# Early products for eight expert pairs, and a step-size projection with its weights held

## The chip, the cores and the metric

The kernel runs on one core of a Trainium2 chip. The metric is the time of one execution on the device in microseconds (us); lower is better. Engines are named as in the profile: PE is TensorE (PEld its weight loads), DVE is VectorE, ACT is ScalarE, POOL is GpSimd, SP is SyncE, which issues most of the transfers.

## The reference

One layer of a diffusion backbone for 640 tokens (128 context tokens, 512 latent ones), model width 1024:

```
h = modulate(rmsnorm(x, norm1), shift1, scale1)
z, xbc, dt_f, dt_b, q, k, v, g_a, g_b = split(h @ w_in)      # dt_f, dt_b: 32 step sizes each
dt = softplus(dt + bias); y_a = ssd_scan(xbc, dt, ...) ; y_b = attention(q, k, v)
x = x + gate1 * (sigmoid(g_a) * y_a + sigmoid(g_b) * y_b) @ w_o
h = modulate(rmsnorm(x, norm2), shift2, scale2)
s = (h @ w_pq) . sub_keys                                    # 8 heads x 2 x 128 scores
gate, idx = softmax of the best 16 sums of a first and a second key, for each head
x = x + gate2 * sum_k gate_k * gelu(h . u_tab[idx_k]) * v_tab[idx_k]   # 16384 experts
y = rmsnorm(x, final_norm)
```

An expert is named by two keys of 128, so 16384 experts are 64 "pairs" of 256 (two first keys, all second keys).

## The kernel before

The program is a row of phases with a barrier between them: modulate, tokens (q, k, v and step sizes), attention, SSD, the merge and output projections, mix_out, route, gates, experts. Weights come from HBM in units of 1 MB (`w_stream`). Each unit is split into a rounded high part (ACT, `w_hi`) and a remainder (DVE, `w_lo`), and a product is three matmuls: high x high, high x low, low x high, all in the chip's rounded 32-bit type (fp32r). Two raw buffers, two high and two low ones take turns.

**modulate and tokens.** In modulate PE transposes the normed tokens, projects the conditioning vector in two halves (L280, `ps_row`), and ACT scales and shifts the transposed tokens tile by tile into `hf` (L207); DVE splits each tile (L221, L223). tokens then begins on PE with the step sizes `t_row`: for each of 5 token tiles and 8 slices of the width three matmuls in which the token tile is the held operand and the 64 columns of weights stream through (L115 to L117, 120 matmuls), and then unit 0 of q, k, v (`t_ps`). DVE's softplus chain (from L535) and ACT's exponentials need all of `t_row`.

**route.** For each of 8 heads h PE makes the queries (`r_ps`, L1848, 96 matmuls) and the scores (`r_pk`, L1858). ACT does, in this order, `copies(h+1)` of the queries (L1889) with the next unit's high part (L100), `score_copies(h)` (`r_sc`, L1898) and `gate_exp(h-1)`: two replicas of the found keys (`r_fr`, L1906) and an exponential (`r_be`, L1911). DVE searches one head after another: two rounds of eight best from the scores (from L1943), the found keys as `r_f` (L1960), the sum candidates, then `r_eq` times `r_fr` (L1985), then `r_be` (L1990), and at the end the low part of the unit of head h+4 (L105).

**gates.** 48 groups of 8 latent tokens become one-hot matrices (DVE, POOL), PE multiplies them into a dense 128 x 128 gate matrix for each token (`e_ps`, L2071), ACT evicts into one of two stages `e_st` of 64 tokens, and SP writes a full stage, 4 MB, to `g_dram` (6 writes, L2039). A stage may be filled again when its write is done.

**experts.** The 384 latent tokens behind the first 256 go through all 64 pairs densely, while the first 256 tokens take their 128 chosen experts each by indirect gathers from HBM, one slot after another: POOL issues `p_uv` (L2188, 256 gathers of 1 MB into a ring of 8), DVE makes the dot product (L2337), and later adds the weighted row to `ysum` (L2351, shown as `merged`, `v_done`). PE alternates `hidden(n+1)` (48 matmuls of 384 columns into `p_pa`) and `output(n)` (36 of 512 columns into six accumulators `p_py`). DVE's step is fixed in the code:

```
dot(n, s, 0, t); weight(n, s); dot(n, s, 1, t)
split_lo(unit_u, 1); w_lo(n, s)          # u of pair n+1; low part of the gated activations
dot(n, s, 2, t); dot(n, s, 3, t)
split_lo(unit_v, 0)                      # v of pair n
slot_weight(n, s, t)
for j in range(GS): take(n, s, j, t)     # GS = 4 slots a pair
```

ACT's split of the v unit waits for `output(n-1)`, since it overwrites that buffer. The gates of a pair are read from `g_dram` as 768 pieces of 512 bytes (L2143). The loops over pairs are hardware loops of two pairs each.

Of the kernel before, what the change touches and what calls it, by code (L numbers as in the profile page):

```python
# [23 lines left out]
P = 128  # L24
# [33 lines left out]
N_EXP = 128  # L58
# [63 lines left out]
def phase_modulate(nc, K, ctx):  # L122
# [9 lines left out]
    hf = sb("hf", [P, 2, KD, P])  # L132
    sq = sb("sq", [P, D])
# [5 lines left out]
    modc = sb("modc", [P, 16, 2])  # L139
    ps_row = ctx.enter_context(nc.psum_tensor("ps_row", [P, 2 * UC], F32))  # L140
# [7 lines left out]
    xn_done = sem("m_xn"); xT_done = sem("m_xT"); hf_done = sem("m_hf"); hhi_done = sem("m_hhi"); hlo_done = sem("m_hlo")  # L148
# [3 lines left out]
    with nc.Block() as block:  # L152
# [32 lines left out]
        def _(act):  # L185
# [5 lines left out]
            for t in range(NT):  # L191
                if t:
                    act.wait_ge(sq_done, t)
                nc.scalar.activation(sq[:, :], xt[:, t, :], ACT.Square, accum_out=ssq[:, t:t + 1]).then_inc(sq_done, 1)
            act.wait_ge(ms_done, 1)
            nc.scalar.activation(rstd[:, :], ssq[:, :], ACT.Sqrt).then_inc(rt_done, 1)
            act.wait_ge(ada_used, 2)
            nc.scalar.activation(row[:, :], ps_row[:, :], ACT.Copy).then_inc(row_done, 1)
            act.wait_ge(scale_done, 4)
            for t in range(NT):  # L200
                for h in range(2):
                    act.wait_ge(xT_done, 2 * t + h + 1)
                    if t >= 2 and h == 0:
                        act.wait_ge(hlo_done, t - 1)
                    for k in range(4):
                        kd = 4 * h + k
                        nc.scalar.activation(hf[:, t % 2, kd, :], ps_x[t % 3][h][:, k, :], ACT.Identity,  # L207
                                             scale=K.mul1[:, kd, group(t):group(t) + 1],
                                             bias=K.add1[:, kd, group(t):group(t) + 1]).then_inc(hf_done, 1)
                if t == 0:  # L210
                    S.hi(act, 0, 0)
                if t == 2:
                    act.wait_ge(dtw_in, 16)
                    nc.scalar.activation(K.whi[1][:, 0:KD * 64], dtw[:, :], ACT.Copy).then_inc(dtw_hi, 1)

        @block.vector
        def _(dve):
            def split(t):

                dve.wait_ge(hf_done, KD * (t + 1))  # L220
                nc.vector.tensor_copy(K.hT[0][:, :, t * P:(t + 1) * P], hf[:, t % 2, :, :]).then_inc(hhi_done, 1)  # L221
                dve.wait_ge(hhi_done, t + 1)
                nc.vector.tensor_tensor(K.hT[1][:, :, t * P:(t + 1) * P], hf[:, t % 2, :, :],  # L223
# [2335 lines left out]
```

## Time and profile before

| | |
|---|---|
| median of 3 runs | 2925.51 us (2924.32 to 2927.39) |
| the profiled execution | 2930.75 us, its span 2929.0 us |
| PE / DVE / ACT / POOL busy, share of the span | 88% / 76% / 39% / 25% |
| experts, by its first and last matmul | 1814.94 to 2907.2 us |
| mean granted clock of PE | 0.93 of full speed |

The span counts from the first to the last instruction; 1.75 us of the execution lie around it. Times below are microseconds from the start of the span. The clock is a share of 2.4 GHz: 1.00 or 0.50.

### The profile page before, as it was taken

Reading aid. Unit: us, or ns where it says so; the run is one execution under the profiler, and the core shown is the slowest. Engines: PE = TensorE matmul, PEld = TensorE weight load, DVE = VectorE, ACT = ScalarE, POOL = GpSimd, SP = SyncE. Lnnn points to the kernel's source line nnn. Section 1 sums busy time; section 2 is a strip of 40 time slices with the busy share of each in tenths; the row PEclk is TensorE's granted clock in tenths of the full one; section 3 lists DMA queues with packets and bytes.
Section 4 is the critical chain, followed back from the end, with each engine's and each line's share of the span. In section 5 each row is a group of like instructions: output and inputs, shape, how many; then the busy total and the mean of one; then the engine's idle time right before and its main releaser. Section 6 shows DMA issues by size and latency. Waiting matters only on the chain. (4 is left out here: it accounts for less than half of the span.)

```text
span 2929.0 us, 41321 instructions
## 1 busy us (share of the span) xinstructions
PE 2562.9 (88%) x15289; PEld 2287.0 (78%) x15289; DVE 2211.7 (76%) x3790; ACT 1144.4 (39%) x1857; POOL 729.5 (25%) x588
## 2 busy tenths in 40 slices
PE   4979999978999998798786078899999999999997
PEld 3967878768887786797686078799899898899896
DVE  2565666661488787433399996899999999999998
ACT  3223445452466565321432176333333333333333
POOL 0000000000456676010000066223323333323221
PEclk7889999999999999899898589999999999999998
DMA  5430211123223231432211036999999999999996
GB/s 231 171 139 17 80 62 66 61 94 112 90 97 118 76 100 61 158 128 106 94 44 37 7 133 260 413 410 403 403 402 396 400 400 398 380 402 397 403 399 242
DMA packets 152003, 614.43 MB, mean 210 GB/s; under 512 B 13344, under 2 KB 77632, under 8 KB 89792
## 3 DMA queue, kind: packets, MB, share of 16 engines
q1 hardware_dynamic: 114720, 344.22, 31.7%
q0 software_dynamic: 36864, 268.45, 22.3%
q8 instruction: 80, 1.31, 0.2%
q14 instruction: 51, 0.42, 0.0%
q10 hardware_dynamic: 288, 0.03, 0.0%
HBM read 556.24 MB, written 56.41 MB: 209 GB/s over the span
## 5 line engine op out<-in xcount | busy, mean ns | idle before, releaser
L2188 POOL DMA_INDIRECT p_uv<-in_uv_rows,merged x256 | 332.7, 1300 | 733.6 <-DVE merged L2351 658.9
L2208 PE MATMUL p_pa<-h2D,w_hi 128*128 128x384 f32 x1024 | 346.7, 339 | 5.9 <-DVE w_lo L2315 3.6
L2210 PE MATMUL p_pa<-h2D,w_lo 128*128 128x384 f32 x1024 | 345.9, 338 | 0.0
L2209 PE MATMUL p_pa<-h2D,w_hi 128*128 128x384 f32 x1024 | 345.7, 338 | 0.0
L2245 ACT ACTIVATE w_hi<-w_raw 128x2048 fp32r<-128x2048 f32 x126 | 241.4, 1916 | 266.1 <-PE p_py L2224 241.0
L2351 DVE SCALAR_TENSOR_TENSOR merged<-p_uv,p_sw,merged 128x1024 f32<-128x1024 f32 x256 | 331.0, 1293 | 9.2
L2337 DVE CUSTOM_DVE_ANT_0 p_uv<-p_uv,merged 128x1024 f32<-128x1024 f32 x256 | 309.8, 1229 | 19.6 <-DMA p_uv<-in_uv_rows,merged 19.6
L2222 PE MATMUL p_py<-w_hi,p_wh 128*128 128x512 f32 x768 | 303.8, 396 | 12.8 <-DVE w_lo L2315 12.8
L2315 DVE TENSOR_TENSOR w_lo<-w_raw,w_hi 128x2048 fp32r<-128x2048 f32 x126 | 288.6, 2290 | 29.1 <-ACT w_hi L2245 29.0
L2223 PE MATMUL p_py<-w_lo,p_wh 128*128 128x512 f32 x768 | 303.4, 395 | 0.0
L2224 PE MATMUL p_py<-w_hi,p_wl 128*128 128x512 f32 x768 | 303.3, 395 | 0.0
L105 DVE TENSOR_TENSOR w_lo<-w_raw,w_hi 128x2048 fp32r<-128x2048 f32 x64 | 153.8, 2404 | 135.0 <-ACT w_hi L100 134.8
L2252 ACT ACTIVATE p_a<-p_pa 128x384 f32<-128x384 f32 x128 | 62.9, 492 | 358.6 <-PE p_pa L2210 358.6
L2208 PEld LDWEIGHTS p_pa<-h2D,w_hi 128*128 128x128 f32 x1024 | 194.0, 189 | 9.5 <-issue 5.6
L790 PE MATMUL c_pp<-hT,w_hi 128*128 128x320 f32 x1024 | 198.6, 316 | 0.0
L2209 PEld LDWEIGHTS p_pa<-h2D,w_hi 128*128 128x128 f32 x1024 | 194.0, 189 | 2.3
L2210 PEld LDWEIGHTS p_pa<-h2D,w_lo 128*128 128x128 f32 x1024 | 193.8, 189 | 0.0
L2222 PEld LDWEIGHTS p_py<-w_hi,p_wh 128*128 128x128 f32 x768 | 144.3, 188 | 45.3 <-DVE w_lo L2315 13.1
L1134 POOL TENSOR_TENSOR s_pv<-s_pv,decay 128x256 f32<-128x256 f32 x48 | 41.5, 865 | 536.2 <-ACT s_st L1295 535.1
L2224 PEld LDWEIGHTS p_py<-w_hi,p_wl 128*128 128x128 f32 x768 | 144.3, 188 | 34.9
L2223 PEld LDWEIGHTS p_py<-w_lo,p_wh 128*128 128x128 f32 x768 | 144.3, 188 | 32.3
L100 ACT ACTIVATE w_hi<-w_raw 128x2048 fp32r<-128x2048 f32 x64 | 122.6, 1915 | 112.4 <-PEq L1563 68.5
(368 smaller groups left out, 6049.6 us busy)
## 6 DMA issues: line engine op xcount, KB each, us to landing
w_raw<-in_w_stream SPq DMA_DIRECT2D x190, 1024.0 KB, 6.8
g_dram<-e_st SPq DMA_DIRECT2D x6, 4096.0 KB, 13.0
p_g<-g_dram SPq DMA_DIRECT2D x64, 384.0 KB, 6.5
t_ada<-in_w_ada SPq DMA_DIRECT2D x16, 1024.0 KB, 10.3
xc_dram<-c_xc SPq DMA_DIRECT2D x8, 1284.0 KB, 4.5
s_xx<-xc_dram SPq DMA_DIRECT2D x8, 642.0 KB, 6.0
s_bc<-xc_dram SPq DMA_DIRECT2D x8, 642.0 KB, 7.7
gate_dram<-s_gst SPq DMA_DIRECT2D x16, 320.0 KB, 6.1
```

What stands on the lines that cost most here:

```text
L790: mm = nc.tensor.matmul(ps_p[:, h, 0:TH], lhs[:, k, cols], rhs[:, k, h * TH:(h + 1) * TH], start=f, stop=l)
L2188: nc.gpsimd.indirect_dma_start(uv[:, k % RING, :], None, K.uv_rows, bass.IndirectOffsetOnAxis(K.sidx[:, t, c:c + 1], 0)).then_inc(K.gather ...
L2208: nc.tensor.matmul(ps_a[m][:, :], wh[:, k, cols], K.h2D[0][:, k, :], start=k == 0, stop=False)
L2209: nc.tensor.matmul(ps_a[m][:, :], wh[:, k, cols], K.h2D[1][:, k, :], start=False, stop=False)
L2210: mm = nc.tensor.matmul(ps_a[m][:, :], wl[:, k, cols], K.h2D[0][:, k, :], start=False, stop=k == KD - 1)
L2222: nc.tensor.matmul(ps_y[o][:, :], Wh[s][:, c, tc], vh[:, c, dc], start=first and c == 0, stop=False)
L2223: nc.tensor.matmul(ps_y[o][:, :], Wh[s][:, c, tc], vl[:, c, dc], start=False, stop=False)
L2224: mm = nc.tensor.matmul(ps_y[o][:, :], Wl[s][:, c, tc], vh[:, c, dc], start=False, stop=last and c == 1)
L2245: nc.scalar.activation(K.whi[slot][:, :], K.raw[slot][:, :], ACT.Copy).then_inc(K.w_hi_done, 1)
L2315: nc.vector.tensor_tensor(K.wlo[slot][:, :], K.raw[slot][:, :], K.whi[slot][:, :].bitcast(F32), ALU.subtract).then_inc(K.w_lo_done, 1)
L2337: nc.vector.tensor_tensor_reduce(uv[:, b, 0:D], uv[:, b, 0:D], K.hrow[:, t, :], 1.0, 0.0, ALU.mult, ALU.add, sa[:, b:b + 1]).then_inc(dot_ ...
L2351: nc.vector.scalar_tensor_tensor(ys[:, t, :], uv[:, b, D:2 * D], sw[:, b:b + 1], ys[:, t, :], ALU.mult, ALU.add).then_inc(v_done, 1)
```

## The change

Four parts.

1. **Step sizes.** The transposed tokens are kept in one tile `xT` (evicted unscaled while the conditioning weights still arrive, then scaled in place slice by slice), DVE splits by slices of the width, and PE projects the step sizes still in modulate, slice by slice, with the 64 weight columns held and 320 tokens streamed: 48 matmuls. tokens begins with 5 transposes of the result.
2. **Early pairs.** Eight pairs (4, 11, ..., 53) leave the stream. Their first products are made in route, two halves of 8 matmuls behind each head's scores, in plain fp32 (`r_pu`, from `ur` and the unsplit tokens `h32`, which mix_out now leaves), with a gelu each on ACT and a trip through `a_dram`. In experts 56 plain pairs remain; after pairs `r` = 4 to 51, in cycles of 6, PE adds 3, 3, 2, 2, 2 and 0 of an early pair's 12 output matmuls (fp32, 512 columns, `p_ve` by `p_ae`).
3. **Slots.** The 256 gather slots are spread over 56 steps: 4 each at the ends, 5, 5, 5, 4, 5, 4 in a cycle. The step's order changes, activations are gated in place, and the hardware loops are unrolled.
4. **Gates by row pairs.** The first 4 of 6 stages are written as 512-byte pieces so that a pair reads them as 2 KB a partition; the last 2 as before. The final gates and norm weights are loaded at the end of experts, not at its start.

```diff
+EARLY = {n: i for i, n in enumerate(range(4, 60, 7))}
+PAIR_OF = [n for n in range(NPAIR) if n not in EARLY]
 # modulate
+            for kd in range(KD):
+                pe.wait_ge(hlo_done, kd + 1)
+                for lhs, rhs, first, last in ((dtwh, K.hT[0], kd == 0, False), (dtwh, K.hT[1], False, False), (dtwl, K.hT[0], False, kd == KD - 1)):
+                    for h in range(2):
+                        mm = nc.tensor.matmul(ps_x[0][h][:, :, :].rearrange("p a c -> p (a c)")[0:64, 0:TH], lhs[:, kd, :],
+                                              rhs[:, kd, h * TH:(h + 1) * TH], start=first, stop=last)
 # tokens
             for t in range(NT):
-                tc = slice(t * P, (t + 1) * P)
-                for kd in range(KD):
-                    mm = mm3(nc, ps_dt[:, t, :], (K.hT[0][:, kd, tc], K.hT[1][:, kd, tc]),
-                             (dtwh[:, kd, :], dtwl[:, kd, :]), kd == 0, kd == KD - 1)
+                mm = nc.tensor.transpose(ps_dt[:, t, :], dtT[0:64, t * P:(t + 1) * P], K.ident[0:64, 0:64])
 # route, PE and ACT
+            for h in range(PH):
+                if h + 1 < PH:
+                    queries(h + 1, (h + 1) % 2)
+                scores(h, h % 2)
+                for i in behind(h):
+                    early_hidden(i)
...
+                    copies(h + 1, (h + 1) % 2)
+                score_copies(h, h % 2)
+                for i in behind(h)[:2]:
+                    early_gelu(i)
+                if h:
+                    gate_exp(h - 1)
 # gates
+                if b < G_PAIRED:
+                    rows = K.g_pairs[:, :, b].rearrange("n j i t -> j n (i t)")
+                    sp.dma_start(rows, stage[b % 2][:, :, :].rearrange("p (n i) t -> p n (i t)", i=2)).then_inc(out[b % 2], 16)
 # experts, PE and DVE
+            for r in range(R):
+                if r + 1 < R:
+                    hidden(r + 1)
+                output(r)
+                if early_of(r) and early_of(r)[1] < CYCLE - 1:
+                    early_output(*early_of(r))
...
+                first = COUNT[r] - 2
+                dot(r, 0)
+                weight(r)
+                dot(r, 1)
+                if r and r < R - 1:
+                    split_lo(u_unit(r + 1))
...
+                for j in range(2, first):
+                    dot(r, j)
+                w_lo(r)
+                slot_weight(r, 0)
+                for j in range(first - 1):
+                    take(r, j)
+                dot(r, first)
+                dot(r, first + 1)
+                if r < R - 1:
+                    split_lo(v_unit(r))
+                take(r, first - 1)
+                slot_weight(r, 1)
+                take(r, first)
+                take(r, first + 1)
```

In route, ACT's order in one head (`r_q` are the queries, `r_sc` the scores, `r_fr` the replicas for the head before, `r_be` its exponential). Before, in the loop:

```order
L1889 ACTIVATE r_q<-r_ps 128x256
L1889 ACTIVATE r_q<-r_ps 128x384
L1889 ACTIVATE r_q<-r_ps 128x256
L1889 ACTIVATE r_q<-r_ps 128x384
L100 ACTIVATE w_hi<-w_raw 128x2048
L1898 ACTIVATE r_sc<-r_pk 128x512 x2
L1898 ACTIVATE r_sc<-r_pk 128x256
L1906 ACTIVATE r_fr<-r_f 128x1280 x2
L1911 ACTIVATE r_be<-r_bs 128x80
```

and of the change, with the replicas of head 0:

```order
L1935 ACTIVATE r_q<-r_psS 128x256
L1935 ACTIVATE r_q<-r_psD 128x384
L1935 ACTIVATE r_q<-r_psS 128x256
L1935 ACTIVATE r_q<-r_psD 128x384
L106 ACTIVATE w_hi<-w_raw 128x2048
L1944 ACTIVATE r_sc<-r_pk 128x512 x2
L1944 ACTIVATE r_sc<-r_pk 128x256
L1964 ACTIVATE r_ua<-r_pu 128x384 x2
L1952 ACTIVATE r_fr<-r_f 128x1280 x2
L1957 ACT_TABLE_LOAD
L1957 ACTIVATE r_be<-r_bs 128x80
```

Two gelus (`r_ua`), whose input `r_pu` PE makes behind the scores, stand ahead of the replicas, and a table load ahead of the exponential; another comes before the next head's gelus.

In experts, DVE's step from the gating to the weighted sums (the rows with ISA are the dot products, `merged` is `ysum`). Before, with its four slots:

```order
L2325 TENSOR_TENSOR p_w<-p_a,p_g 128x384 x2
L2337 ISA p_uv,p_sa<-p_uv,merged 128x1024
L2337 ISA p_sa 128x1
L2315 TENSOR_TENSOR w_lo<-w_raw,w_hi 128x2048
L2331 TENSOR_TENSOR p_wl<-p_w,p_wh 128x768
L2337 ISA p_uv,p_sa<-p_uv,merged 128x1024
L2337 ISA p_sa 128x1
L2337 ISA p_uv,p_sa<-p_uv,merged 128x1024
L2337 ISA p_sa 128x1
L2315 TENSOR_TENSOR w_lo<-w_raw,w_hi 128x2048
L2342 TENSOR_TENSOR p_sw<-p_sg,merged 128x4
L2351 SCALAR_TENSOR_TENSOR merged<-p_uv,p_sw,merged 128x1024 x4
```

and of the change, in the first step of a cycle (five slots), from the split of the u unit on:

```order
L2399 TENSOR_TENSOR w_lo<-w_raw,w_hi 128x2048
L2428 ISA p_uv,p_sa<-p_uv,merged 128x1024
L2428 ISA p_sa 128x1
L2421 TENSOR_TENSOR p_wl<-p_a,p_wh 128x768
L2435 TENSOR_TENSOR p_sw<-p_sg,merged 128x3
L2445 SCALAR_TENSOR_TENSOR merged<-p_uv,p_sw,merged 128x1024 x2
L2428 ISA p_uv,p_sa<-p_uv,merged 128x1024
L2428 ISA p_sa 128x1
L2428 ISA p_uv,p_sa<-p_uv,merged 128x1024
L2428 ISA p_sa 128x1
L2399 TENSOR_TENSOR w_lo<-w_raw,w_hi 128x2048
L2445 SCALAR_TENSOR_TENSOR merged<-p_uv,p_sw,merged 128x1024
```

Two of the weighted sums now stand between the two splits, and the slots are weighted in two parts (`p_sw` of 3, and of 2 behind this piece). Ahead of this step the early pair was gated.

## Rows read from the trace of the kernel before

**Rows 1.** The page: the span.
```profile
span 2929.0 us, 41321 instructions
```

**Rows 2.** Windows: busy time, clock, DMA share and GB/s of two stretches.
```profile
core 0: us, PE busy (x) PEld busy (x) DVE busy (x) ACT busy (x) POOL busy (x), PEclk, DMA share, GB/s
61.00:87.00 26.00, 25.87 (x121) 25.90 (x122) 0.77 (x2) 1.54 (x2) 3.96 (x9) 0.50 0.47 184
1846.00:2895.00 1049.00, 1045.26 (x5229) 942.29 (x5230) 1010.70 (x1129) 353.06 (x374) 331.06 (x250) 1.00 1.00 398
```

**Rows 3.** Waits from 1846 to 2895 us: total, times, longest.
```profile
DVE w_lo L2315 <- ACT w_hi L2245: 29.0, 60, 2.3
ACT w_hi L2245 <- DMA w_raw<-in_w_stream: 25.1, 19, 3.0
```

**Rows 4.** Timeline of PE: begin of a hidden and of the output behind it.
```profile
2207.83 0.34 PE L2208 MATMUL p_pa<-h2D,w_hi 128*128 128x384 f32 x1
...
2216.16 0.39 PE L2222 MATMUL p_py<-w_hi,p_wh 128*128 128x512 f32 x1
```

**Rows 5.** Timeline of DVE, one step of experts and the next step's begin.
```profile
2200.91 1.22 DVE L2337 CUSTOM_DVE_ANT_0 p_uv<-p_uv,merged 128x1024 f32<-128x1024 f32 x1
2202.06 1.02 DVE L2325 TENSOR_TENSOR p_w<-p_a,p_g 128x384 f32<-128x384 f32 x2
...
2204.14 2.29 DVE L2315 TENSOR_TENSOR w_lo<-w_raw,w_hi 128x2048 fp32r<-128x2048 f32 x1
...
2212.46 5.25 DVE L2351 SCALAR_TENSOR_TENSOR merged<-p_uv,p_sw,merged 128x1024 f32<-128x1024 f32 x4
...
2217.62 1.22 DVE L2337 CUSTOM_DVE_ANT_0 p_uv<-p_uv,merged 128x1024 f32<-128x1024 f32 x1
```

**Rows 6.** Timeline of PE, DVE and ACT in modulate and at the begin of tokens.
```profile
61.13 0.39 PE L115 MATMUL t_row<-w_hi,hT 128*128 128x64 f32 x1 [12.78 <-PEq L2432]
86.72 0.56 PE L115 MATMUL t_ps<-w_hi,hT 128*128 128x256 f32 x1
56.99 1.23 DVE L223 TENSOR_TENSOR hT<-hf,hT 128x1024 fp32r<-128x1024 f32 x1
39.68 2.90 ACT L207 ACTIVATE hf<-ps_x,add,mul 128x128 f32<-128x128 f32 x8 [1.68 <-DVE mul L246]
```

**Rows 7.** Timeline of PE: plain fp32 matmuls (two records each).
```profile
246.85 1.34 PE L748 MATMUL a_ps<-KT,QT 64*128 64x320 f32 x4
1459.82 1.39 PE L1858 MATMUL r_pk<-r_keys,r_q 128*128 x11
1476.14 2.39 PE L1858 MATMUL r_pk<-r_keys,r_q 128*128 x20
```

**Rows 8.** Timeline of DVE and ACT in route: heads 0 and 5.
```profile
1465.57 2.02 DVE L1943 MAX8 r_v<-r_sc 128x8 f32<-128x128 f32 x10
1482.09 2.48 ACT L1906 ACTIVATE r_fr<-r_f 128x1280 bf16<-128x1280 bf16 x2
1487.55 1.49 DVE L1985 TENSOR_TENSOR r_eq<-r_eq,r_fr 128x2560 bf16<-128x2560 bf16 x1
1607.86 2.02 DVE L1943 MAX8 r_v<-r_sc 128x8 f32<-128x128 f32 x10
```

**Rows 9.** Critical chain in gates: two groups of 8 tokens.
```profile
1798.42 2.02 PE e_ps L2071 x16
...
1800.69 2.02 PE e_ps L2071 x16
```

**Rows 10.** DMA queue from 1183 to 1187 us: one write in 1 KB pieces.
```profile
q1 hardware_dynamic: 144, 0.13, 9.7%
```

**Rows 11.** DMA queues from 2000 to 2400 us: packets, MB, share of 16 engines.
```profile
q0 software_dynamic: 13824, 100.67, 61.2%
q1 hardware_dynamic: 25547, 59.48, 40.0%
```

**Rows 12.** The page: a DMA queue that carries instructions.
```profile
q8 instruction: 80, 1.31, 0.2%
```

More of the change, by code:

```diff
@@ L202, in _ @@
                     act.wait_ge(xT_done, 2 * t + h + 1)
[L203 to L209, printed above, removed]
@@ L1847, in queries @@
                             for h, part in enumerate((K.h2S, K.h2D)):
-                                mm = nc.tensor.matmul(ps[2 * m + h][:, :], lhs[:, k, cols], part[r][:, k, :], start=first, stop=last)
+                                mm = nc.tensor.matmul(ps[2 * m + h], lhs[:, k, cols], part[r][:, k, :], start=first, stop=last)
                 mm.then_inc(mm_done, 1)
@@ L2211, in hidden, with output @@
                     mm.then_inc(a_mm, 1)
-            def output(n, s, slot, unit):
-                pe.wait_ge(K.w_lo_done, unit + 1)
-                pe.wait_ge(wl_done, n + 1)
-                first, last = isinstance(n, int) and n == 0, isinstance(n, int) and n == PAIRS - 1
+            def output(r):
+                s, slot = r % 2, slot_of(v_unit(r))
+                pe.wait_ge(K.w_lo_done, v_unit(r) + 1)
+                pe.wait_ge(wl_done, r + 1)
+                first, last = r == 0, r == R - 1
                 vh, vl = (x[slot][:, :].rearrange("p (c d) -> p c d", c=2) for x in (K.whi, K.wlo))
@@ L2241, in _, with split_hi @@
+            EARLY_ORDER = [(o, c) for o in range(len(OUTS)) for c in range(2)]
+            hidden(0)
+            for r in range(R):
+                if r + 1 < R:
[3 more added lines that the diff above has]
+                    early_output(*early_of(r))
         @block.scalar
         def _(act):
-            def split_hi(unit, slot):
+            def split_hi(unit):
+                slot = slot_of(unit)
                 act.wait_ge(K.w_loaded[slot], (unit - slot + 2) * 8)
@@ L2353, in step @@
-            def step(n, s, t, unit_u, unit_v, slot_v=0):
-                dot(n, s, 0, t)
-                weight(n, s)
-                dot(n, s, 1, t)
-                if unit_u is not None:
-                    split_lo(unit_u, 1)
-                w_lo(n, s)
-                dot(n, s, 2, t)
-                dot(n, s, 3, t)
-                if unit_v is not None:
-                    split_lo(unit_v, 0)
-                slot_weight(n, s, t)
-                for j in range(GS):
-                    take(n, s, j, t)
```

480 lines of the change are left out of this document (266 added, 214 removed).

## Prediction

> **What bounds the kernel now.** I read the windows first. In experts, 1846 to 2895 us, PE is busy 1045 of 1049 us at full clock, DVE 1011, and the 16 DMA engines all the time, at 398 GB/s [rows 2]. Three things are nearly full, so the timeline has to say which one sets the pace. On PE hidden runs from 2207.83 and output starts at 2216.16: 8.33 us for 48 matmuls, 0.174 each [rows 4]. DVE's step starts at 2200.91 and the next at 2217.62: the period is 16.70 us [rows 5], which leaves 8.37 us for 36 matmuls of 512 columns, 0.233 each. PE has no gap, so it sets the period. DVE's own wait in the waits view is 29.0 us in 60 steps, 0.48 a step [rows 3]: its work is 16.2 us of 16.70. ACT waited for weight loads 19 times, 25.1 us in all [rows 3], and nobody waited for that in turn. 64 periods are 1069 us of the span of 2929.0 [rows 1].
>
> At the begin PE is also full, but at half clock: the step sizes take from 61.13 to 86.72, 25.6 us for 120 matmuls, clock 0.50 [rows 2, 6]. Route is bound by DVE: from head 0 at 1465.57 to head 5 at 1607.86 are 28.46 us a head [rows 8]; PE uses 16.3 us of that (scores at 1459.82 and at 1476.14) [rows 7]. In gates a group of 8 tokens takes 2.27 us, so a stage of 64 fills in 18.2 [rows 9].
>
> **Step sizes.** The 120 matmuls leave tokens; 5 transposes stay, some 1.4 us. In modulate the new order is a pipeline by slices. ACT starts scaling at 39.68 as before; 8 operations of 128 columns took 2.90, 0.36 each [rows 6], I take 0.55 for one of 512: 0.9 a slice, under DVE's pace. DVE's subtraction of 1024 columns takes 1.23 [rows 6]; for 640 I take 0.8 and 0.46 for the copy, 1.27 a slice, 10.2 for eight, and 2.2 for unit 0's low part between them. DVE is done at 40.6 + 12.4 = 53.0, PE's last six matmuls and ACT's two copies bring it to 55.7; before, DVE ended at 56.99 + 1.23 = 58.2 and PE began 2.9 later [rows 6]. So tokens starts at 58.6, unit 0 at 59.9 and not 86.7: **-27**. What follows in tokens waits for PE or for DVE's softplus chain, which moves along. The transposes now run on while the second half of the conditioning weights arrives; that may keep the clock up in L280: -1 more. Bounds: -20 (the ada loads then become late) to -31.
>
> **Route.** Each head gets 16 more matmuls of 384 columns in plain fp32. Four records of 320 columns, two matmuls, took 1.34 us with their tail [rows 7]; 20 records of 128 columns took 2.39, 0.239 a matmul. That is 4 passes: 0.70 for 384 columns, 11.2 us a head. PE then needs 16.3 + 11.2 = 27.5 to 27.9 a head, just under DVE's 28.46: in the long run it hides. But ACT's queue has the gelus ahead of the replicas. Head 0's replicas stand behind the gelus of head 1. PE: queries of head 2 from 1473.4 (after the first early pair) to 1487.7, scores of 1 to 1490.1, early products 2 and 3 to 1501.3, gelu 1501.8, replicas 2.4 more: **1504.3**. DVE wants them 22.0 us after its begin, at 1487.55, and had them at 1484.6 [rows 8]. DVE waits 17 us. Walking on with 27.9 for PE and 28.46 for DVE, head 1 begins at 1510.8 and wants its replicas at 1532.8; they are there at 1532.2. Later heads have more in hand. So the stall is paid once: **+17**. Bounds: 0 (if it were hidden) to +25 (if each head loses a little more).
>
> **Gates.** Four writes of 4 MB now consist of 512-byte pieces, 512 for each DMA engine. None such is in the trace. A write in 1 KB pieces cost 9.7% of 64 engine-us for 144 packets, 43 ns each, at most 49 if only its 128 data pieces count [rows 10]. Reads of 512 bytes: in 400 us the SP queue took 40.0% of 6400 engine-us [rows 11]; the 50 MB of weights in it at 26 bytes a ns are 1917, the other 643 belong to 18,400 pieces, 35 ns each. Bounds for a write: 20 ns (its bytes at full rate), W = 10 us a stage, and 49 ns, W = 25. The stage after next may be filled when the write is done, so with all four slow the delay at the last stage is 4W - 70 if that is positive. Nearest row is the read: 36 ns, W = 18.6, **+4**. Upper bound: +30. The Trainium skill (DMA: Bandwidth & Descriptors, latency and other measured facts) gives 207 GB/s for copies whose rows lie 512 KiB apart and less for wider pitches; here the pieces of a partition lie 256 KiB apart, and by an estimate from that rate a stage takes 20 us, +11; no run here shows it yet.
>
> **Experts.** Eight periods of 16.70 go, -134 us. The early output matmuls are fp32 of 512 columns, 4 x 0.233 = 0.93 each, 12 a pair, 11.2 us: +90. On PE a cycle of 6 plain and one early pair is 100.2 + 11.2 = 111.4 us, where 7 pairs took 116.9; eight cycles and eight plain pairs are 1025 and not 1069: -44. DVE: a step of four slots is 16.2 plus a second weighting of slots 0.2, a fifth slot is a dot of 1.15 (2202.06 - 2200.91) and a sum of 1.31 (a quarter of 5.25) [rows 5]; a cycle has 28 slots and one gating of 0.9: 6 x 16.4 + 4 x 2.46 + 0.9 = 109.1, under PE. The wait of 0.48 in it has slots between the splits to cover it. Without that cover DVE would be at 112.
>
> Transfers: for each 7 pairs they fall from 46.8 MB to 46.1 (12 units, one early v, 0.4 MB of activations, 7 gate rows, 28 gathers). At 398 GB/s [rows 2] that is 115.9 us, longer than PE's 111.4. But the gates of a pair are 384 packets and not 768. By the packet prices (gathers 25.7 bytes a ns for an engine, weights 26, 512 bytes 35 ns, 2 KB some 85) a cycle takes 113.7 us at a share of 1.00; the trace reached 61.2 + 40.0 = 101.2% [rows 11], 112.4 us. I take **112.5**: 8 x 112.5 + 134 = 1034, **-35**. The start of the phase has 0.9 MB more in the queue while DVE waits for gathers: **+2**. The end is unchanged: the same step, and the final weights are loaded behind the last splits.
>
> **Sum.** -28 + 17 + 4 - 35 + 2 = -40, against the profiled 2930.75: 2890.75. The median of the runs shown is 5.2 us lower, so 2885.5, 1.4% faster. A run can't tell 0.2%, 6 us, from no change.
>
> **Rivals.**
> - *The transfers are the bound (20 in 100).* For it: share 1.00 at 398 GB/s now [rows 2]. Against: nobody but ACT waits for a load today [rows 3], and the pieces get larger. If 398 GB/s is a ceiling, 8 x 115.9 + 134 = 1061, -8 in experts, and the time is 2912; with half of that, 2899.
> - *The paired writes hold up gates (12 in 100).* At 49 ns a piece +30 instead of +4: 2911. The skill's pitch rule above would do the same by another cause, 2893 by its rate.
> - *No stall at head 0 (8 in 100).* If the replicas came in time: 2868. Against it speaks the order of ACT's queue.
> - *Slower: the unrolled code is not fetched in time (8 in 100).* PE's 56 steps are some 9400 instructions, with 64 bytes each 0.6 MB. Queue q8 moved 1.31 MB in 80 packets, 16 KB each, so there are 37 packets more in the one phase where the DMA engines are full; before, the loop sat still there. 0.2% of 46,900 engine-us over 80 are 1.2 us a packet [rows 12]. If PE stood still longer than 40/37 = 1.1 us at each, the gain would be gone; at 1.6 us it costs 59 and the time is 2944. Against: phases that are unrolled already have almost no such gap on PE.
> - The Trainium skill (Runtime: NRT & Kernel Launch, instruction fetch mechanics) says the next block is fetched while the current one runs and that taken branches are what breaks this; by it the unrolled code costs nothing. No run here shows that under full DMA load.
>
> **How the numbers follow.** The forecast holds 52 in 100, by itself 2872 to 2898. 2858 to 2914 takes in the missing stall, the full ceiling of transfers and the upper write price, and leaves out the fetch case and mixtures of two bad ones. Faster by over 0.2%: 0.87; within it 0.05; slower 0.08.
>
> **What the profile after would show.** First `t_ps` at about 60 us (-27 right if between 57 and 62). In route one wait of DVE for `r_fr` of 14 to 20 us at head 0 and none after; the phase some 17 us longer. In gates the time between stages stays near 18.2 us; 25 would be the write rival. In experts, 111 to 113.5 us a cycle with PE busy 98% or more; if DVE waits for `p_uv` or ACT for `w_raw` by more than 100 us in all, the transfers bind; if PE shows gaps put down to issue, the code does. The forecast is wrong if tokens gives back the 27 us later, at the ada loads (they had some 2 us in hand), or if PE's fp32 matmuls cost more than 0.93.

## The result and the profile after

| | before | changed |
|---|---|---|
| median | 2926.45 us (4 runs, 2924.32 to 2940.38) | 2881.28 us (4 runs, 2880.41 to 2883.04) |
| profiled execution, its span | 2930.75, 2929.0 us | 2883.04, 2881.3 us |

The ratio is 0.9836, with a 95% interval of 0.9806 to 0.9867: 1.6% faster, 45 us by the medians, 47.7 us by the spans. The forecast was 2885.5.

The account is read from the first matmul of each phase in both traces:

| | before | changed | difference so far |
|---|---|---|---|
| first q, k, v matmul (`t_ps`) | 86.72 | 57.85 | -28.9 |
| first matmul of attention | 214.84 | 192.33 | -22.5 |
| first queries in route | 1427.4 | 1402.0 | -25.4 |
| first `e_ps` in gates | 1698.6 | 1688.2 | -10.4 |
| first hidden in experts | 1814.94 | 1804.60 | -10.3 |
| end of the span | 2929.0 | 2881.3 | -47.7 |

So tokens gives 6.4 us of its gain back, 2.9 come back in the phases between attention and route (their code is the same in both kernels), route costs 15, gates nothing, and experts bring 37.4.

**tokens.** The timeline of PE and of DVE in the changed kernel (start, duration, then the operation; in brackets the idle time before it and what ended it):

```profile
57.85 0.58 PE L121 MATMUL t_ps<-w_hi,hT 128*128 128x256 f32 x1
78.37 0.63 PE L653 MATMUL t_pt<-dtA,tri_le 128*128 128x160 f32 x1 [4.15 <-DVE dtA L566]
```
```profile
66.45 0.76 DVE L546 COPY q_ckd<-q_ck 128x256 f32<-128x256 f32 x2 [14.74 <-DMA q_ck<-in_cache_k]
67.13 0.48 DVE L550 TENSOR_TENSOR xdt<-t_row,dt_bias 128x320 f32<-128x320 f32 x1
...
77.83 0.49 DVE L566 TENSOR_TENSOR dtA<-dt,nega 128x320 f32<-128x320 f32 x1
```

The q matmuls start 28.9 us earlier than in [rows 6]. But the softplus chain, 11 us long as before, starts only 19.9 us earlier: ahead of it in DVE's queue stand two copies of cached keys whose transfer lands at 66.45. In the kernel before the same copies were over long before the chain could start:

```profile
69.35 0.77 DVE L531 COPY q_ckd<-q_ck 128x256 f32<-128x256 f32 x2 [11.13 <-DMA q_ck<-in_cache_k]
87.02 0.49 DVE L535 TENSOR_TENSOR xdt<-t_row,dt_bias 128x320 f32<-128x320 f32 x1 [16.90 <-PE t_row L117]
```

In the changed kernel unit 0 on PE ends at 74.2, and PE waits 4.15 us for the chain. The windows show what follows the gap (columns as in [rows 2]): the clock is 0.70 on average and not 1.00.

```profile
78.00:86.30 8.30, 7.65 (x76) 4.74 (x77) 4.56 (x5) 2.83 (x3) 0.00 (x0) 0.70 0.37 128
```

**route.** The timeline of DVE and of ACT at heads 0 and 1, against [rows 8]:

```profile
1440.32 2.02 DVE L1995 MAX8 r_v<-r_sc 128x8 f32<-128x128 f32 x10
...
1476.87 1.49 DVE L2037 TENSOR_TENSOR r_eq<-r_eq,r_fr 128x2560 bf16<-128x2560 bf16 x1 [14.62 <-ACT r_fr L1952]
1483.36 2.03 DVE L1995 MAX8 r_v<-r_sc 128x8 f32<-128x128 f32 x10
...
1511.87 2.02 DVE L1995 MAX8 r_v<-r_sc 128x8 f32<-128x128 f32 x10
```
```profile
1473.96 0.49 ACT L1964 ACTIVATE r_ua<-r_pu 128x384 f32<-128x384 f32 x1 [4.67 <-PE r_pu L1906]
1474.34 2.42 ACT L1952 ACTIVATE r_fr<-r_f 128x1280 bf16<-128x1280 bf16 x2
```

One wait, at head 0, 14.62 us; from head 1 on the heads are again 28.5 apart (1483.36, 1511.87). ACT had just left the second gelu of head 1. PE's scores of heads 0 and 1 began at 1434.58 and 1461.20: 26.62 us a head, under DVE's 28.46.

**gates.** The page's list of transfers, with the median time from issue to landing:

```profile
g_pairs<-e_st SPq DMA_DIRECT2D x4, 4096.0 KB, 16.1
...
g_late<-e_st SPq DMA_DIRECT2D x2, 4096.0 KB, 12.1
```

A paired write takes 4 us longer than a whole-row one and still lands before the 18.1 us in which the next stage fills. Nothing waits for it.

**experts.** Windows of the middle of experts:

```profile
1960.00:2740.00 780.00, 773.47 (x3683) 661.80 (x3682) 745.23 (x894) 247.22 (x294) 310.84 (x196) 1.00 1.02 412
```

and the timeline of PE: the first hidden of a cycle, its first three early matmuls, the hidden behind them, and the first hidden of the next cycle:

```profile
1904.04 0.34 PE L2298 MATMUL p_pa<-h2D,w_hi 128*128 128x384 f32 x1
...
1920.75 2.74 PE L2325 MATMUL p_py<-p_ve,p_ae 128*128 128x512 f32 x6
1922.92 0.74 PE L2298 MATMUL p_pa<-h2D,w_hi 128*128 128x384 f32 x1
...
2014.62 0.34 PE L2298 MATMUL p_pa<-h2D,w_hi 128*128 128x384 f32 x1
```

This cycle takes 110.58 us. Three of the eight, this one among them, take that long; the others take up to 113.6, and the eight end at 2798.23: 894.2 us, 111.8 on average. The longer ones stand behind a weight unit. Here it is on ACT and then on PE:

```profile
2160.74 1.91 ACT L2342 ACTIVATE w_hi<-w_raw 128x2048 fp32r<-128x2048 f32 x1 [6.92 <-DMA w_raw<-in_w_stream]
```
```profile
2165.03 0.44 PE L2298 MATMUL p_pa<-h2D,w_hi 128*128 128x384 f32 x1 [0.78 <-DVE w_lo L2399]
```

The waits view of 1960 to 2740 (total, times, longest) has more of it than [rows 3]:

```profile
ACT w_hi L2342 <- DMA w_raw<-in_w_stream: 65.4, 26, 7.7
```

Two places at the ends are new. At the begin the second output of PE waits behind a late weight unit:

```profile
1859.96 0.79 PE L2313 MATMUL p_py<-w_hi,p_wh 128*128 128x512 f32 x1 [4.96 <-DVE w_lo L2399]
```
```profile
1855.67 1.91 ACT L2342 ACTIVATE w_hi<-w_raw 128x2048 fp32r<-128x2048 f32 x1 [12.67 <-DMA w_raw<-in_w_stream]
```

At the end POOL gates the first token tile, and two DVE operations beside it take 2.35 and 3.52 us (POOL first, then DVE):

```profile
2845.52 3.03 POOL L2282 TENSOR_TENSOR merged<-merged,w_raw 128x1024 f32<-128x1024 f32 x1 [19.80 <-DMA w_raw<-gates]
2848.63 2.40 POOL L2284 TENSOR_TENSOR merged<-merged 128x1024 f32<-128x1024 f32 x1
```
```profile
2846.22 2.35 DVE L2435 TENSOR_TENSOR p_sw<-p_sg,merged 128x2 f32<-128x2 f32 x1
2848.60 3.52 DVE L2445 SCALAR_TENSOR_TENSOR merged<-p_uv,p_sw,merged 128x1024 f32<-128x1024 f32 x1
```

### The profile page after: what moved, and what is told of

Its sections match the earlier page's. It is cut to its first block and busy times, and to the rows that moved or that the text cites. A ratio compares the mean times of both kernels' runs of the same rounds, so it can differ in the third digit from the quotient of the medians.

```text
span 2881.3 us, 39222 instructions
## 1 busy us (share of the span) xinstructions
PE 2571.6 (89%) x14998; PEld 2225.5 (77%) x14998; DVE 2165.3 (75%) x3820; ACT 1133.2 (39%) x1880; POOL 811.8 (28%) x620
## 5 line engine op out<-in xcount | busy, mean ns | idle before, releaser
L2278 POOL DMA_INDIRECT p_uv<-in_uv_rows,merged x256 | 398.0, 1555 | 632.4 <-DVE merged L2445 571.7
L2298 PE MATMUL p_pa<-h2D,w_hi 128*128 128x384 f32 x896 | 317.3, 354 | 5.7 <-DVE w_lo L2399 3.4
L2300 PE MATMUL p_pa<-h2D,w_lo 128*128 128x384 f32 x896 | 302.2, 337 | 0.0
L2299 PE MATMUL p_pa<-h2D,w_hi 128*128 128x384 f32 x896 | 302.2, 337 | 0.0
L2313 PE MATMUL p_py<-w_hi,p_wh 128*128 128x512 f32 x672 | 268.1, 399 | 19.7 <-DVE w_lo L2399 19.7
L2399 DVE TENSOR_TENSOR w_lo<-w_raw,w_hi 128x2048 fp32r<-128x2048 f32 x110 | 251.6, 2287 | 37.6 <-ACT w_hi L2342 37.5
L2342 ACT ACTIVATE w_hi<-w_raw 128x2048 fp32r<-128x2048 f32 x110 | 210.4, 1912 | 168.5 <-DMA w_raw<-in_w_stream 86.5
L2314 PE MATMUL p_py<-w_lo,p_wh 128*128 128x512 f32 x672 | 266.9, 397 | 0.0
L2315 PE MATMUL p_py<-w_hi,p_wl 128*128 128x512 f32 x672 | 266.8, 397 | 0.0
L111 DVE TENSOR_TENSOR w_lo<-w_raw,w_hi 128x2048 fp32r<-128x2048 f32 x64 | 153.8, 2404 | 135.8 <-ACT w_hi L106 135.5
L2298 PEld LDWEIGHTS p_pa<-h2D,w_hi 128*128 128x128 f32 x896 | 169.3, 189 | 18.4 <-issue 11.0
L2299 PEld LDWEIGHTS p_pa<-h2D,w_hi 128*128 128x128 f32 x896 | 169.4, 189 | 9.1 <-issue 8.6
L801 PEld LDWEIGHTS c_pp<-hT,w_hi 128*128 128x128 f32 x1024 | 160.9, 191 | 0.2
L853 DVE TENSOR_REDUCE a_nmax<-a_ps 128x1 f32<-128x640 f32 (+1 forms) x80 | 57.3, 717 | 131.0 <-PE a_ps L759 113.3
## 6 DMA issues: line engine op xcount, KB each, us to landing
t_ada<-in_w_ada SPq DMA_DIRECT2D x16, 1024.0 KB, 10.3
g_pairs<-e_st SPq DMA_DIRECT2D x4, 4096.0 KB, 16.1
```

Source lines behind the costliest of these rows:

```text
L801: mm = nc.tensor.matmul(ps_p[:, h, 0:TH], lhs[:, k, cols], rhs[:, k, h * TH:(h + 1) * TH], start=f, stop=l)
L2278: nc.gpsimd.indirect_dma_start(uv[:, k % RING, :], None, K.uv_rows, bass.IndirectOffsetOnAxis(K.sidx[:, t, c:c + 1], 0)).then_inc(K.gather ...
L2298: nc.tensor.matmul(ps_a[m][:, :], wh[:, k, cols], K.h2D[0][:, k, :], start=k == 0, stop=False)
L2299: nc.tensor.matmul(ps_a[m][:, :], wh[:, k, cols], K.h2D[1][:, k, :], start=False, stop=False)
L2300: mm = nc.tensor.matmul(ps_a[m][:, :], wl[:, k, cols], K.h2D[0][:, k, :], start=False, stop=k == KD - 1)
L2313: nc.tensor.matmul(ps_y[o][:, :], Wh[s][:, c, tc], vh[:, c, dc], start=first and c == 0, stop=False)
```

## Experiments

Each is the changed kernel with the edit shown, if nothing else is said. Medians stand beside 2881.28. The kernel before, timed beside each group of experiments, had medians of 2926.1 to 2928.0, so differences between groups carry some 2 us of scatter.

### Replicas ahead of the gelus

```diff
+                if h:
+                    gate_exp(h - 1)
-                for i in behind(h)[:2]:
+                for i in behind(h):
                     early_gelu(i)
-                if h:
-                    gate_exp(h - 1)
```

> The changed kernel with one thing moved in route: ACT makes the replicas and the exponential of head h-1 before the gelus of head h's early products, as the order was before the change. Against the changed kernel's 2881.3 us. Theory (DVE's wait of 14.62 us for the replicas of head 0 comes only from the gelus ahead of them in ACT's queue): that wait goes, all heads of DVE are 28.46 us apart, the kernel takes 14.6 us less, 2867. Rival (the early products themselves crowd PE and ACT, and the wait only shows at the replicas): with the gelus now late, PE waits for a free accumulator of the early products or DVE for its scores, and less than 5 us is gained: 2876 or more.

Measured: 2874.34 us, 7 less. From the first 384-column query matmul to the first `e_ps` it took 277.1 us in place of 285.8. DVE's wait is not gone:

```profile
1467.37 1.49 DVE L2035 TENSOR_TENSOR r_eq<-r_eq,r_fr 128x2560 bf16<-128x2560 bf16 x1 [6.12 <-ACT r_fr L1952]
1473.86 2.02 DVE L1993 MAX8 r_v<-r_sc 128x8 f32<-128x128 f32 x10
```

ACT's timeline shows what now stands right ahead of the replicas, the copies of the scores of head 1; ahead of those come the copies of the next queries, for which ACT had waited until 1460.49:

```profile
1463.57 1.39 ACT L1944 ACTIVATE r_sc<-r_pk 128x512 f32<-128x512 f32 x3
1464.79 2.48 ACT L1952 ACTIVATE r_fr<-r_f 128x1280 bf16<-128x1280 bf16 x2
```

PE makes those queries and scores behind the early products of head 0. So 8.5 us of the stall belong to the gelus and 6.1 to the copies of queries and scores. Neither theory of the expectation had this.

### Replicas ahead of everything that waits for PE

```diff
+                if 1 <= h <= 4:
+                    replicas(h - 1)
                 if h + 1 < PH:
                     copies(h + 1, (h + 1) % 2)
                 score_copies(h, h % 2)
```

> As the run with the replicas ahead of the gelus, and in addition the replicas of heads 0 to 3 stand ahead of the copies of the queries and of the scores, which wait for PE. With the replicas only ahead of the gelus DVE still waited 6.12 us for them: they stood behind score copies whose matmuls come after the early products and the next queries on PE. Theory: that wait goes too, route takes 14.6 us less than in the changed kernel and 6 less than in the run before, 2867. Rival: ACT now waits for DVE's found keys with the copies of the queries behind it, PE gets its queries later and DVE waits for scores: 2873 or more.

Measured: 2869.68 us, 11.6 less. DVE's only wait in the heads is now for the exponential:

```profile
1464.18 0.24 DVE L2043 TENSOR_REDUCE r_sm<-r_be 128x5 f32<-128x80 f32 x1 [2.13 <-ACT r_be L1958]
```

The phase took 273.2 us, 12.6 less: the stall was a matter of ACT's order alone. Counted alike, the kernel before takes 270.8; what the early products still cost is that one wait. Experts took 4.1 us longer than in the changed kernel (1080.8 against 1076.7 from the first hidden to the end), which is not explained.

### Softplus chain first

```diff
-            dve.wait_ge(ck_in, 16)
-            for c in range(2):
-                nc.vector.tensor_copy(ckd[:, :, c, :], heads(ck[:, :])).then_inc(ck_done, 1)
...
             S.lo(dve, 1, 1)
+            dve.wait_ge(ck_in, 16)
+            for c in range(2):
+                nc.vector.tensor_copy(ckd[:, :, c, :], heads(ck[:, :])).then_inc(ck_done, 1)
```

> The changed kernel with one thing moved in tokens: DVE's two copies of the cached keys, which wait for a transfer until 66.45 us, stand behind the softplus chain and the split of unit 1 and no longer ahead of them. Theory (the chain starts late because of the queue, and PE's gap of 4.15 us behind unit 0 and the half clock behind that gap follow from it): the chain starts when the biases are there, at about 63.1, PE has no gap at 74 us, attention begins 6 us earlier, and the kernel takes 6.3 us less, 2875. Rival (the conditioning weights' transfers, which now have to come 29 us earlier, set the pace in tokens): the gap is replaced by a wait for them, less than 2 us is gained.

Measured: 2877.73 us, 3.6 less. The chain starts at 62.46, when the last of its parameters lands, PE's wait is 1.11 us, and attention begins at 185.88 where it was 192.33:

```profile
62.46 0.49 DVE L547 TENSOR_TENSOR xdt<-t_row,dt_bias 128x320 f32<-128x320 f32 x1 [10.92 <-DMA nega<-in_a_log_b]
```
```profile
74.19 0.54 PE L653 MATMUL t_pt<-dtA,tri_le 128*128 128x160 f32 x2 [1.11 <-DVE dtA L563]
```

The mechanism holds, and the transfers did not take its place. Its size is smaller than this one pair of traces says. From the first `t_ps` to the first matmul of attention it takes 128.6 to 130.2 us in the four kernels of this document that have the chain first, and 130.6 to 134.8 in the nine others with the new tokens: 3.4 us less on average. The medians say 3.6, but this kernel's four executions lie between 2875.3 and 2882.4, so they alone could hardly tell it.

The scatter goes with the clock. In the 8.3 us behind PE's gap it was 0.66 to 0.80 in seven of the nine, but 1.00 in the other two, with gaps of 2.6 and 3.2 us, and 1.00 in all four with the chain first, with gaps of 0.7 to 1.5 us. So the half clock behind the gap is no fixed price of it.

### Step sizes alone

The kernel before, with modulate and tokens of the changed kernel.

> The kernel before with the first part of the change alone: modulate and tokens are those of the changed kernel, all else is as before. Attention begins 20 to 23 us earlier (in the changed kernel 22.5, of 28.9 at the first q matmul), and if nothing behind tokens takes it back, the whole kernel takes 22 to 25 us less than before: 2902 to 2904. If experts and the phases between give the gain back, less than 18.

Measured: 2899.33 us against 2928.04 for the kernel before beside it, ratio 0.9900 (0.9875 to 0.9924): 29 us, somewhat more than forecast. By the traces 23.3 us are there at the first matmul of attention, as forecast; 6.4 more come until the first queries of route, in phases whose code is the same in both kernels (SSD took 388.1 us where it had taken 391.8, and it differs so between other traces too, see the end). Nothing behind tokens takes the gain back.

### Less work for PE

```diff
-                for o, c in EARLY_ORDER[PART[i]:PART[i + 1]]:
+                for o, c in EARLY_ORDER[PART[i]:PART[i] + 1]:
```

> The changed kernel, but PE makes only 5 of the 12 output matmuls of each early pair; the transfers, the gatings and all else stay. Left out: most of eight experts pairs' second products. PE's cycle of 6 plain pairs and one early falls from 110.6 to about 104.6 us. If PE sets the pace, the cycle falls until DVE binds at some 109 us, from the mean of 111.8 now: 8 x 2.7 = 22 us less, 2860. If the transfers are the bound (46.1 MB a cycle at the 412 GB/s that they reach), the cycles stay at 111.5 to 112, PE shows the difference as idle time, and the kernel takes 0 to 3 us less.

Measured: 2878.64 us (one run), 2.6 less. The eight cycles took 111.3 us on average, and PE idled in them:

```profile
1960.00:2740.00 780.00, 745.77 (x3580) 648.46 (x3579) 744.30 (x892) 244.25 (x294) 309.87 (x196) 0.99 1.02 411
```

```profile
ACT w_hi L2342 <- DMA w_raw<-in_w_stream: 124.8, 33, 10.1
```

PE had 48 us less to do in the eight cycles, and they took 4 us less. Something other than PE holds the cycle at 111 to 112 us; the waits say the transfers, and the next run tests it.

### Fewer bytes

```diff
-                sp.dma_start(VE[p % 2][:, :, :].rearrange("p c d -> p (c d)"), K.v_early[p]).then_inc(ve_in[p % 2], 16)
+                part = slice(0, 2 * D if p < 2 else 16)
+                sp.dma_start(VE[p % 2][:, :, :].rearrange("p c d -> p (c d)")[:, part], K.v_early[p][:, part]).then_inc(ve_in[p % 2], 16)
```

> The changed kernel, but from the third early pair on only 64 bytes of each partition's 8 KB of its second weights are loaded: 6 MB less in 48 packets' place a pair, PE's work unchanged. Left out: the right weights of six early pairs. If the 9.5 us by which eight cycles take longer than 8 x 110.6 are waits for transfers, the six cycles concerned come down to 110.6 us each and the kernel takes 7 to 9 us less, 2873; ACT's waits for raw weights shrink from 65 us in cycles 2 to 8 to under 20. If PE, DVE or the order of their steps cause them, nothing changes: within 2 us of 2881.

Measured: 2869.4 us (one run), 11.9 less. All eight cycles took 110.6 us (1899.9 to 2784.6), ACT waited 3.9 us for raw weights from 1960 to 2740 where it had waited 65.4, and PE had no idle time:

```profile
1960.00:2740.00 780.00, 780.00 (x3731) 671.09 (x3730) 754.32 (x903) 246.79 (x297) 314.33 (x199) 1.00 1.01 409
```

Of the 13.6 us between the two spans, 7.0 lie between the first hidden and the end, as forecast; the other 6.7 came ahead of it, in phases with the same code. Both runs together: PE asks for 110.6 us a cycle, the transfers for 111 to 112, and the larger one is seen. DVE, which the prediction put at 109.1, had the same work in both.

### The old format of the gates

```diff
-G_PAIRED = 4
+G_PAIRED = 0
```

(and a pair's gates read by one transfer, from `g_late`)

> The changed kernel with the gates' old format: all six stages written in 16 KB pieces, every pair read as 768 pieces of 512 bytes. Against the changed kernel's 2881.3. The other runs show that transfers limit experts now (with 6 MB less all cycles took 110.6 us, with less work for PE they stayed). By the packet prices of the prediction (35 ns for a 512-byte read, some 85 for 2 KB) a pair's gates cost 768 x 35 ns = 26.9 engine-us in place of 256 x 35 + 128 x 85 = 19.8, 0.44 us a pair more, 3.1 a cycle, 24 to 28 us in all: 2906. If only bytes count in the transfers' limit, nothing changes in experts: 2881. Gates: 0 either way, since a stage takes 18.1 us to fill and its write lands in 16.1.

Measured: 2906.35 us, 25 more. The cycles take 114.8 us on average, with less moved at the same share of the DMA engines:

```profile
1960.00:2740.00 780.00, 758.51 (x3574) 652.22 (x3573) 720.88 (x864) 237.34 (x284) 298.96 (x189) 0.98 1.01 399
```

This is the prediction's packet arithmetic put to the test, and it holds: the bytes of a cycle are the same, only their pieces differ. By the traces all of the loss lies in experts (1100.8 us against 1076.7); gates takes as long as before. The 398 GB/s of [rows 2] was a ceiling for those pieces and not for the DMA engines. Queue q1 from 2000 to 2400 us, of this run and then of the changed kernel:

```profile
q1 hardware_dynamic: 26771, 59.28, 39.3%
```
```profile
q1 hardware_dynamic: 18258, 60.69, 38.2%
```

This run also splits the gain. It holds the step sizes, the early pairs and the new slots, but not the row pairs, and it is 7 us slower than the step sizes alone (2899.33, timed beside the same executions of the kernel before). By the traces route costs 15.0 us more than there and experts bring 11.7; the rest lies in phases with the same code. So with the old format the early pairs, at this order of ACT's queue, do not pay: they take work from PE, and the transfers hold the cycle at 114.8 us. They pay because the row pairs lighten the transfers.

### Five stages in pairs

```diff
-G_PAIRED = 4
+G_PAIRED = 5
```

> The changed kernel with 5 of the 6 stages written as row pairs, where 4 were: the last stage alone is written in whole rows. By the packet prices (512 bytes 35 ns; a piece grows from 2 to 2.5 KB for some 20 ns) a pair costs 128 x 35 - 128 x 20 ns = 1.9 engine-us less, 0.12 us a pair, 6 to 8 us in 56 steps as long as transfers are the limit: 2874. If only bytes count: 2881. If the fifth paired write is in the way at the end of gates (it lands 4 us later than a whole-row one, but a full stage of 18 us before the last), up to 2 us more.

Measured: 2873.06 us, 8.2 less. The cycles take 111.2 on average, five of the eight 110.6, at 414 GB/s, and experts 7.0 us less, as the packet prices say. From the first `e_ps` to the first hidden it took 116.4 us, as with four stages: the fifth paired write is hidden too.

### Early loads later

```diff
-            load_hidden(0)
-            load_early(0)
-            load_early(1)
             for r in range(R):
...
+                if r == 2:
+                    load_hidden(0)
+                    load_early(0)
+                if r == 6:
+                    load_early(1)
```

> The changed kernel, with the first loads of early activations and second weights (2.4 MB, 5.8 us at 415 GB/s) issued behind the weight loads of pairs 2 and 6, and not ahead of the loop; they are used from 1920 us on. In the changed kernel the second output of PE came 24.1 us after the first hidden behind it, where 16.7 is the rule, with ACT waiting 12.67 us for a weight unit. Theory (these loads push that unit back): the begin of experts gets 5 to 7 us shorter. What becomes of it is open: if the transfers are full all the way to the first early pair, the 5.8 us return as waits in the next cycles and the whole kernel gains under 2 us, 2880; if the plain pairs, which need 395 GB/s, leave room for them, it keeps 5: 2876.

Measured: 2886.23 us, 5 more. The gap of 4.96 us at the begin is gone, but the two steps up to the first early matmuls are longer (23.3 and 20.5 us), and behind them PE is exactly where it was: 118.3 us from the first hidden to the second step of the first cycle, in both kernels. So the loads' time returned in full, as the first half of the expectation has it. The rest of the trace's loss lies in the cycles (5.3 us more in eight, counted from that step) and is not explained: one of the moved loads falls in them, 1 MB or 2.4 us at 412 GB/s, and kernels with the same experts differ by up to 3.1 us there. The four executions lie between 2881.4 and 2890.7, and the traced one is the slowest of them, so the size of the loss is uncertain.

### Together

The four changes that were meant to save time; then also the tail on DVE; then without the moved loads.

> The changed kernel with four changes of the other runs together: the replicas ahead of PE's work in ACT's queue (11.6 us by medians), the softplus chain first (3.6), five paired stages (8.2) and the early loads behind the first weights. If they add up: 2881.3 - 23.4 and 0 to 5 for the loads, 2853 to 2858. If the starting transfers of experts limit them jointly (experts took 4 us longer in each kernel that reached it earlier), 2860 to 2864. The Trainium skill is not needed for this sum.

```diff
# POOL
-            nc.gpsimd.tensor_tensor(ys[:, 0, :], ys[:, 0, :], gate2[:, group(0), :], ALU.mult).then_inc(gated0, 1)
-            pool.wait_ge(gated0, 1)
-            nc.gpsimd.tensor_tensor(res[0], res[0], ys[:, 0, :], ALU.add).then_inc(summed0, 1)
# DVE, behind its last weighted sum
+            nc.vector.tensor_tensor(ys[:, 0, :], ys[:, 0, :], gate2[:, group(0), :], ALU.mult).then_inc(gated0, 1)
+            dve.wait_ge(gated0, 1)
+            nc.vector.tensor_tensor(res[0], res[0], ys[:, 0, :], ALU.add).then_inc(summed0, 1)
```

> As the run of the four changes together, but the gating and the residual sum of the first token tile at the end are done by DVE (two operations, 1.23 us each) and not by POOL. In the changed kernel, while POOL did them (2845.5 to 2851.0), two operations of DVE took 2.35 and 3.52 us, where they take 0.15 and 1.28 elsewhere, and DVE bounds the end. If POOL's work is what slows DVE: 4.4 - 2.5 = 1.9 us less than the run of the four. If the slow operations have another cause: 2.5 us more.

The last kernel is this one with the early loads back where the changed kernel has them (the edit of the section above undone).

> The last run (replicas ahead, softplus first, five paired stages, the tail on DVE), but with the early loads where the changed kernel has them, since moving them cost about 5 us (2886.2 against 2881.3), and the four together came to 2861 and not to the sum. If the moved loads also cost 5 here: 2858.7 - 5 = 2854. If their cost is gone because fewer packets leave room: 2857 to 2860.

Measured: 2860.98, 2858.73 and **2855.69** us, in this order. The last is 0.9754 of the kernel before (0.9735 to 0.9773), 2.5% faster, and 25.6 us better than the changed kernel. The parts that it holds had brought 11.6, 3.6 and 8.2; with some 2 for the tail they would give 25.4. The first is what its expectation gives for a joint limit, but that cause is not shown: the 4 us by which experts were to be longer in kernels that reach it earlier are 2.3 to 4.1 in the traces of the three that do. The last step, the loads moved back, brought 3.0 us by the medians, less than the 5 that moving them had cost. The tail of the second, where DVE does what POOL did:

```profile
2830.57 0.15 DVE L2433 TENSOR_TENSOR p_sw<-p_sg,merged 128x2 f32<-128x2 f32 x1
2830.76 1.29 DVE L2443 SCALAR_TENSOR_TENSOR merged<-p_uv,p_sw,merged 128x1024 f32<-128x1024 f32 x1
```

From the last output matmul's start to the end it takes 22.5 us, where the first has 24.8: 2.3 us less, the same two operations being fast again. By the medians alone (2860.98 and 2858.73, each with a spread of 11 or 12 us) this could not be told.

## Why the prediction was right, and where not

**Step sizes, -28 forecast, -25.4 at route.** Up to `t_ps` the pipeline was right and 2 us too slow (57.85, not 59.9). The sentence that failed is "DVE's softplus chain, which moves along". In the kernel before DVE sat idle in front of it, so that a copy ahead of it in the queue, waiting for a transfer, cost nothing and was not looked at. Of the 6.4 us that tokens gave back, 3.4 hang on the chain, by the average of all traces; 1.6 stay with the chain first (129.7 us from `t_ps` to attention against 128.1), which is not explained, and the rest is this trace's scatter. At attention the term is -22.5 and its miss 5.5 us. That it looks like 2.6 at route is luck: the 2.9 us between come from phases whose code the change did not touch (below).

**Route, +17 forecast, +15.0.** One stall at head 0 and none after it, as worked out. Two errors in it. An early matmul of 384 columns takes (26.62 - 16.32) / 16 = 0.64 us and not 0.70, which makes the stall 2 us shorter. And only 8.5 us of it hang on the gelus that the prediction named; the other 6.1 come from the copies of queries and scores, which the same early products delay.

**Gates, +4 forecast, 0.** The write of 512 pieces a DMA engine landed in 16.1 us, at most 31 ns a piece, where the price of a read, 36, was taken. The prediction's 4W - 70 is then negative and nothing is waited for. By the rate of the Trainium skill (DMA: Bandwidth & Descriptors, latency and other measured facts), 207 GB/s at a row pitch of 512 KiB, the prediction had an estimate of 20 us; 4.19 MB in 16.1 us are 260 GB/s with the latency in it. The page's rows are 16 KiB for each partition, while here the pieces of one partition lie 256 KiB apart, so this run neither bears the rule out nor refutes it.

**Experts with their start, -33 forecast, -37.4.** Four terms:
- Eight cycles: -41.3 (8 x 116.94 to 894.2) and not -35. The price of PE was too high: 12 early matmuls take 110.58 - 6 x 16.71 = 10.3 us, 0.86 each, not 0.93. The transfers, taken at 112.5 by the packet prices, needed 111.8 on average. The mechanism, transfers a little longer than PE, was right, and it is settled by the three runs that changed PE's work, the bytes, and the pieces.
- Two long steps in the kernel before, 19.7 us from 2475 and 19.6 from 2495, which I did not see: -6. There POOL gated and summed the first token tile in the middle of experts, and DVE beside it was slow: four weighted sums took 7.27 us where they take 5.25 [rows 5], a dot product 3.42 where it takes 1.22, and PE waited (POOL, DVE, PE):

```profile
2483.21 2.75 POOL L2193 TENSOR_TENSOR merged<-merged,p_g 128x1024 f32<-128x1024 f32 x1
2486.03 3.27 POOL L2195 TENSOR_TENSOR merged<-merged 128x1024 f32<-128x1024 f32 x1
```
```profile
2479.77 7.27 DVE L2351 SCALAR_TENSOR_TENSOR merged<-p_uv,p_sw,merged 128x1024 f32<-128x1024 f32 x4
2486.96 3.42 DVE L2337 CUSTOM_DVE_ANT_0 p_uv<-p_uv,merged 128x1024 f32<-128x1024 f32 x1
```
```profile
2494.81 0.68 PE L2208 MATMUL p_pa<-h2D,w_hi 128*128 128x384 f32 x1 [2.81 <-DVE w_lo L2315]
```

  In the 19.6 us behind that gap the granted clock was 0.84 on average, where it is 1.00 in the step after, and PE was busy all the time. The change moved POOL's two operations to the end and so took this cost away.
- The start: +7 and not +2. From the first hidden to the hidden of pair 3 it was 58.8 us and is now 66.0; the early loads stand in the queue ahead of a weight unit. With them moved it was 56.0, but the time came back two steps later.
- The end: +2.6 and not 0. The prediction said "the same step" and missed that POOL's two operations had moved there. The first slow row of DVE ends with POOL's first (2848.57 and 2848.55), the second 1.1 us behind POOL's second (2852.12 and 2851.03), and the dot product above 1.1 us behind POOL's too (2490.38 and 2489.30): DVE seems to stand still until POOL is done. The run without POOL's work agrees. The Trainium skill (Advanced Engine Details and Errata, VectorE performance modes) says that POOL shares DVE's second port to SBUF and that its instructions and DVE's two-port ones block each other; its table gives tensor_tensor no two-port mode, and here a tensor_tensor took 2.35 us instead of 0.15 all the same.

The cycles and the long steps brought 12 us more than forecast, the start and the end 8 less, and neither was foreseen: that the whole of experts is off by only 4.4 us is in part luck.

**The rivals.** The transfers are in fact the bound, but at 112 us a cycle and not at 115.9: the rival's mechanism with the price of the old pieces. The slow write did not occur. The unrolled code cost nothing: q8 moved 119 packets (80 in [rows 12]), and the waits view of experts puts none of PE's matmul gaps down to issue, and of its weight loads none longer than 0.2 us, but for the first one of the phase (2.4 us). That agrees with the rule of the Trainium skill (Runtime: NRT & Kernel Launch, instruction fetch mechanics) that the next block is fetched while the current one runs, here under full DMA load. One sign of the prediction was set wrong: it wanted ACT to wait more than 100 us in all for raw weights if the transfers bind; they bind, and ACT waited 86.5.

So the terms were off by +2.6, -2.0, -4 and -4.4 us. They sum, but for rounding, to the 7.7 between -40 and the -47.7 of the spans. The medians lie 45 apart, since the traced execution of the kernel before was 4.3 us above its median and that of the changed one 1.8.

## What to carry to other kernels

- When a wait goes, look along the engine's queue for instructions that stood in its shadow. Two copies of cached keys and the replicas were harmless until the work behind or ahead of them moved: 3.4 us in tokens and 12.6 in route. In an in-order queue, put what the critical engine wants ahead of what waits for a busy one.
- When transfers are full, count pieces as well as bytes. 512-byte rows stored by pairs and read as 2 KB are worth 25 us here, more than half the gain of the whole change, without one byte less. Without them the early pairs would have cost 7 us, with less work on PE: a saving on one engine counts only once the next limit is out of its way.
- When two limits lie about 1% apart (110.6 and 111.8), lighten each by itself: less work for PE gave next to nothing, fewer bytes gave the whole difference, and that tells which one binds.
- An elementwise operation on POOL is not free for DVE: two of them cost 6 us in the middle of experts and 2.6 at its end. Where DVE is nearly full, look at its rows beside POOL's.

## What the runs showed of the hardware that I had not expected

- A phase with the same code differs from trace to trace by steps of about 3 us: in fourteen traces, each of another kernel, SSD took 388, 391 or 394.5 us, within 0.8. The granted clock goes with it, 0.97 in one of 388 us and 0.94 in one of 394 (windows of the changed kernel, then of the run with the replicas ahead of the gelus):

```profile
762.00:1151.00 389.00, 354.28 (x2210) 302.46 (x2209) 310.62 (x439) 229.66 (x561) 253.06 (x232) 0.97 0.27 89
```
```profile
758.00:1153.00 395.00, 362.04 (x2208) 309.12 (x2206) 310.06 (x438) 229.67 (x561) 252.61 (x232) 0.94 0.27 88
```

What sets it off is not known. It is enough to hide an effect of 3 us between two traces.
- The share of the DMA engines was 1.01 to 1.02 in all kernels, while 398 to 415 GB/s were moved between 1960 and 2740 us: a share of 1 says that the engines are occupied, not how much gets through.
- A plain fp32 matmul of 512 columns took 0.86 us, 3.7 times the 0.233 of one of the rounded type with its weight load. The prediction had taken four times.
- An operation of DVE that met one of POOL's took some 2 us longer (0.15 to 2.35, 1.28 to 3.52, 1.22 to 3.42 us) and ended with it or 1.1 us behind it.
